# Statistic rows of stage 3: one split operand and one product of 64 rows for each spread, in place of a product of 5 fp32 rows

## The reference, cut to what matters

```python
o = _rmsnorm(o, gla_norm_g) * silu(r)          # each of 4 heads of 128 channels by itself
u = silu(_layernorm(conv(u), conv_ln_g, conv_ln_b))   # 512 channels
x = x + gt1 * concat([o, u]) @ w_out
h = _rmsnorm(x, norm_ffn_g) * (1 + sc2) + sh2   # then router logits, then the experts
```

## Time and profile before

| | us |
|---|---|
| median of 3 runs | 2720.18 |
| the three runs | 2714.88, 2720.18, 2720.66 |
| the profiled execution, its own time | 2712.45 |
| span of its instructions | 2709.8 |
| stage 3, from about 848 to 1322 in the span | 474 |

### The profile page before, as it was taken

How to read it: one execution, slowest core, us unless ns; L and a number is a source line. 1 busy time by engine, 2 the same in 40 slices (tenths; PEclk the granted TensorE clock), 3 DMA queues, 4 the chain that set the end, 5 groups by cost and what they waited for, 6 DMA issues and landing times.

```text
span 2709.8 us, 41042 instructions
## 1 busy us (share of the span) xinstructions
PE 2461.4 (91%) x15405; PEld 2166.3 (80%) x15405; DVE 1624.5 (60%) x2729; ACT 1208.0 (45%) x1946; POOL 782.2 (29%) x686
## 2 busy tenths in 40 slices
PE   5679989999997889999649999999999999999994
PEld 1667868688785566777418999999999999999994
DVE  0575949679496453342464666665566666665575
ACT  3555355464423233323115555555544555555553
POOL 1020010101000031101012554445555544445451
PEclk9879989999997879889658999999999999999997
DMA  5884565665545446432444766667777666666875
GB/s 194 304 289 159 172 214 190 232 199 183 198 164 204 132 140 163 121 113 84 128 87 141 207 194 191 192 184 205 198 199 206 194 195 195 183 196 198 285 230 202
DMA packets 287074, 505.61 MB, mean 187 GB/s; under 512 B 31614, under 2 KB 230107, under 8 KB 271098
## 3 DMA queue, kind: packets, MB, share of 16 engines
q1 hardware_dynamic: 247562, 377.84, 42.4%
q0 software_dynamic: 39408, 126.38, 17.8%
HBM read 405.63 MB, written 98.53 MB: 186 GB/s over the span
## 4 chain that ended last, share of the span: by engine, by line
PE 77%; DVE 6%; ACT 4%; DMA 3%; issue 2%; POOL 2%; SPq 0%; DVEq 0%; ACTq 0%; POOLq 0%
PE bank L1423 22%; PE bank L1425 22%; PE bank L1424 22%; PE bank L1606 2%; PE bank L1544 1%; DVE work_out L2079 1%; PE bank L1672 1%; PE bank L1637 1%; PE bank L1583 1%; PE bank L1571 1%; DVE work_exp L2272 1%; ACT work_proj L747 1%; PE bank L1663 1%; DMA out_dram<-work_exp 1%; PE bank L1484 1%
## 5 line engine op out<-in xcount | busy, mean ns | idle before, releaser
L1423 PE MATMUL bank<-act_hl_exp,hl_exp 128*128 128x288 f32 x3072 | 913.0, 297 | 38.3 <-POOL act_hl_exp L1341 25.3
L1424 PE MATMUL bank<-act_hl_exp,hl_exp 128*128 128x288 f32 x3072 | 909.2, 296 | 0.0
L1425 PE MATMUL bank<-act_hl_exp,hl_exp 128*128 128x288 f32 x3072 | 907.5, 295 | 0.0
L1423 PEld LDWEIGHTS bank<-act_hl_exp,hl_exp 128*128 128x128 f32 x3072 | 579.0, 188 | 42.0 <-issue 30.3
L1425 PEld LDWEIGHTS bank<-act_hl_exp,hl_exp 128*128 128x128 f32 x3072 | 581.3, 189 | 0.0
L1424 PEld LDWEIGHTS bank<-act_hl_exp,hl_exp 128*128 128x128 f32 x3072 | 580.2, 189 | 0.0
L2390 DVE TENSOR_TENSOR hl_exp<-work_exp,hl_exp 128x1024 fp32r<-128x1024 f32 x192 | 231.7, 1227 | 226.4 <-ACT hl_exp L1030 226.4
L2390 DVE TENSOR_TENSOR hl_exp<-raw_exp,hl_exp 128x1024 fp32r<-128x1024 f32 x192 | 232.3, 1225 | 201.9 <-ACT hl_exp L1030 201.9
L2032 DVE SCALAR_TENSOR_TENSOR work_proj<-work_proj,wcv 128x392 f32<-128x392 f32 (+11 forms) x600 | 343.2, 644 | 0.0
L1030 ACT ACTIVATE hl_exp<-work_exp 128x1024 fp32r<-128x1024 f32 x192 | 199.5, 1055 | 217.8 <-PE bank L1425 212.6
L1030 ACT ACTIVATE hl_exp<-raw_exp 128x1024 fp32r<-128x1024 f32 x192 | 198.6, 1052 | 166.4 <-PE bank L1425 166.4
(11 more groups left out here) (320 smaller groups left out, 3642.8 us busy)
## 6 DMA issues: line engine op xcount, KB each, us to landing
hl_proj<-park_w POOLq DMA_DIRECT2D x80, 1024.0 KB, 5.5
raw_exp<-in_w_e_gate_dram SPq DMA_DIRECT2D x32, 1024.0 KB, 5.7
raw_exp<-in_w_e_up_dram SPq DMA_DIRECT2D x32, 1024.0 KB, 5.7
work_exp<-in_w_e_gate_dram SPq DMA_DIRECT2D x32, 1024.0 KB, 6.2
work_exp<-in_w_e_up_dram SPq DMA_DIRECT2D x32, 1024.0 KB, 5.8
raw_exp<-in_w_e_down_dram SPq DMA_DIRECT2D x32, 1024.0 KB, 5.6
work_exp<-in_w_e_down_dram SPq DMA_DIRECT2D x32, 1024.0 KB, 5.7
park_w<-hl_proj SPq DMA_DIRECT2D x10, 2048.0 KB, 12.5
```

The costliest lines, as they stand in the source:

```text
L1423: pe.matmul(out, lh, rh, start=first, stop=False)
L1424: pe.matmul(out, lh, rl, start=False, stop=False)
L1425: return pe.matmul(out, ll, rh, start=False, stop=last_)
```

## The change

ACT copies the five reciprocals as fp32r (high part) to rows 0 to 4 of a 64-row tile, and DVE writes what the copy left out (low part) to rows 32 to 36. The other rows are zero. The stationary operand of product h has ones in rows h and 32 + h (`spread_sel`), so that one fp32r product adds both parts; before it was a product of two fp32 operands of 5 rows. The tile lies in `reset`, which POOL clears for it at the start of stage 3. `spread` waits for the low part instead of the reciprocals. The rest of the diff moves counts of the semaphore `r_sel`.

```diff
+        spread_rs = reset.bitcast(f32r)[0:64, 0:BT]
+        spread_sel = reset.bitcast(f32r)[0:64, BT:BT + 5]
...
+        r_sh, r_sl = s_zt.again(0), s_z.again(0)
...
+            def stat_hi(m):
+                act.wait_ge(r_rc, m + 1)
+                wait_pos(act, r_bc, 5 * m)
+                if m == 0:
+                    act.wait_ge(r_sel, 7)
+                act.activation(spread_rs[0:5, 0:T3[m]], W3["rs"][0:5, 0:T3[m]], ACT.Copy).then_inc(r_sh.sem, 1)
...
                 if prep:
                     stat_roots(prep)
+                    stat_hi(prep)
                 if NT3[m] == 4:
                     evict(g0 + 1)
...
+            pool.memset(reset[0:64, 0:2 * BT], 0.0).then_inc(r_sel, 1)
             pool.memset(W3["selc"], 0.0).then_inc(r_sel, 1)
-            pool.wait_ge(r_sel, 1)
+            pool.wait_ge(r_sel, 2)
...
             def spread(m):
-                pe.wait_ge(r_rc, m + 1)
+                upto(pe, r_sl, m + 1)
...
-                    pe.matmul(psum[6 + h % 2][:, 0:T3[m]], ident[0:5, h:h + 1].broadcast_to([5, 128]), W3["rs"][0:5, 0:T3[m]], start=True,
-                              stop=True).then_inc(r_bc, 1)
+                    pe.matmul(psum[6 + h % 2][:, 0:T3[m]], spread_sel[:, h:h + 1].broadcast_to([64, 128]),
+                              spread_rs[:, 0:T3[m]], start=True, stop=True).then_inc(r_bc, 1)
...
-                pe.wait_ge(r_sel, 6)
+                pe.wait_ge(r_sel, 7)
...
                 dve.reciprocal(rs, rs).then_inc(r_rc, 1)
+                upto(dve, r_sh, m + 1)
+                dve.tensor_tensor(spread_rs[32:37, 0:T3[m]], rs, spread_rs[0:5, 0:T3[m]].bitcast(f32), ALU.subtract)\
+                   .then_inc(r_sl.sem, 1)
...
             def prologue():
+                dve.tensor_tensor(spread_sel, ident[0:64, 0:5], ident[0:64, 32:37], ALU.add)
```

More of the change, by code:

```diff
@@ L372, in hybrid_layer @@
         e_dn, e_yt, e_yev, e_sc = sem("e_dn"), sem("e_yt"), sem("e_yev"), sem("e_sc")
-        e_mod, e_row = Sig(r_sel, 0, 0, 6), Sig(r_nst, 0, 0, 16)
+        e_mod, e_row = Sig(r_sel, 0, 0, 7), Sig(r_nst, 0, 0, 16)
         e_u = sem("e_u")
@@ L383, in hybrid_layer @@
         f_s3 = Sig(k_m, 0, 0, 33)
-        f_q, f_g = Sig(k_cnt, 0, 0, CNT_IL + 3), Sig(r_sel, 0, 0, 6 + 96)
+        f_q, f_g = Sig(k_cnt, 0, 0, CNT_IL + 3), Sig(r_sel, 0, 0, 7 + 96)
         f_gl = sem("f_gl")
@@ L972, in prologue @@
                 stat_roots(0)
+                stat_hi(0)
                 cat_his(0)
```

## The result

The changed kernel takes 2697.02 us (median of 8 runs, 2689.96 to 2705.06), the kernel before 2716.47 us in 8 runs beside it. The ratio is 0.9934, 95% interval 0.9917 to 0.9951: about 18 us faster, where 10.6 us (0.9961) had been forecast and 2701 was the low end of the range. The first three runs of the kernel before, on whose median of 2720.18 the forecast was built, were 3.7 us slower than the median of all eight.

The account below looks back on a forecast made before the run. PE bounds the kernel, its chain covering 77% of the span. Blocks 2 to 4 gain 8.2 us with three falls, block 1 1.6; three falls 9.8, two 11.4, middle 10.6: 2720.18 - 10.6 = 2709.6 us, range 2701 to 2718.

Parts of the forecast that it names:

- the old stretch: Blocks 2 to 4, from the spread's first product to the router behind it: 12.13, 13.55 and 13.58 us before.
- I expect one fall behind it in two or three of the three blocks: Blocks 2 to 4: clock drops to 1.2 GHz behind the new 3.2 us spread; total gain 9.8 to 11.4 us, chance 0.60.
- first rival: Blocks 2 to 4: the clock stays up; gain 14.5 us, giving 2705.7 us; chance 0.15.
- the middle of the forecast: Whole kernel: 10.6 us gain, between 9.8 with three falls of the clock and 11.4 with two.
- Block 1: Split uncovered: first product 1.4 us later, last scaling 1.5 earlier, parked states cap the gain at 1.7; 1.6 us taken.
- That a product of 64 rows takes what one of 128 does: Each new fp32r spread product takes 0.23 us, the figure for 128 rows; bounds 0.23 and 0.43.
- The split is covered: Blocks 2 to 4: copy and subtraction, 1.4 us, finish 1.0 us before PE asks for the low part.
- Block 0: Split adds about 0.8 us, products give about as much back, ahead of a 10.55 us wait for parked states: zero.
- Clearing the tile: POOL at the start of stage 3: 0.9 us, upper bound 1.8, ahead of a wait for a DMA: zero.
- ACT's chain: Behind the spread: silus, copies and `token` run 10.7 us until PE's `row_T`; the gain is handed on.
- The clock by rule: Skill's rule that long idle gaps drop the clock: new spread's gaps, under 0.7 us, would keep it; the old trace disagrees.

Follow-up runs that it names:

- the split alone: Kernel before plus the split, made and waited for but unused; each spread still a product of 5 fp32 rows from the reciprocals: ratio 1.0008.
- The padded kernel: Kernel before with its five fp32 rows written into a cleared tile of 64 rows, without the split: ratio 0.9972.
- the woven run: Changed kernel with the five spread products laid between the 24 products of the projection behind, blocks 2 to 4: 2698.79 us, ratio 0.9943.
- the tucked run: Changed kernel with 128 rows, products 0 and 1 ahead of the transposes, 2 to 4 each behind three projection products: 2707.90 us, ratio 0.9918.

## Why the prediction was wrong, point by point

**Where the gain lies.** All in stage 3. Three profiles of each kernel:

| | stage 3, us | its start, us | stretches of blocks 2, 3, 4, us |
|---|---|---|---|
| before | 473.9, 484.2, 479.6 | 848.5, 844.5, 842.1 | 12.13, 13.55, 13.58; 12.14, 15.21, 15.21; 13.57, 13.55, 13.56 |
| after | 459.5, 457.0, 466.0 | 839.8, 845.9, 840.4 | 8.70, 8.67, 10.25; 8.67, 8.67, 10.26; 8.70, 8.68, 8.67 |

The means are 479.3 and 460.8: 18.5 us, which is the whole measured difference; outside stage 3 the three spans of each kernel differ by 2 us in the mean (2243.7 and 2241.6). The start scatters in both, and in the eight profiles of the other kernels, with the same code ahead of it (841.7 to 848.1).

**The step that failed: sizing the old stretch from one execution.** The 12.13 us of block 2 and the 13.55 and 13.58 of blocks 3 and 4 were right for that execution and mild for the kernel. Over nine stretches the mean is 13.6, with two of 15.2. The prediction had seen that a fall of the clock costs 1.5 us or 3, and did not ask how often the costly case comes; it had one execution, but three of three stretches with a fall should have opened the range on the side of a larger gain.

**The step beside it: "I expect one fall behind it in two or three of the three blocks", because PE is idle for two thirds.** There was one in two of nine (10.25 and 10.26). Idle time alone was the wrong thing to look at. The count of rows of the products counts too, as the kernels side by side show:

| product | rows | stretches with a fall in the spread or right behind it |
|---|---|---|
| two fp32 instructions | 5 | 12 of 12 (three profiles of before, one of the split alone) |
| two fp32 instructions | 64 | 0 of 6 |
| one fp32r | 5 | 2 of 3 |
| one fp32r | 64 | 2 of 9 |
| one fp32r | 128 | 0 of 6 |

The three stretches of a profile are not independent draws. For fp32 the times confirm the table: both kernels with 64 rows are faster than the kernel before beyond their intervals. For fp32r the counts are too small to tell 5 rows from 64 or 64 from 128. So the forecast's first rival, the clock staying up, was nearly what happened, at 2 of 9. Its words "products of 64 rows in place of 5" named the cause without giving it the weight.

**What each step is worth.** Blocks 2 to 4 gave 14.9 us (mean time from the start of the spread of block 2 to the end of stage 3: 294.4 before, 279.5 after), where the middle of the forecast had 9.0 (8.2 with a fall in each, 12.9 with none). The stretches hold 3 x (13.61 - 9.03) = 13.7 of it. Of these 4.7 above the forecast, 1.6 are the old stretches (40.8 us for three, not 39.3) and 2.9 the falls that did not come (0.7 in an execution, not 2.5, at 1.6 each); the remainder is rounding (the forecast's three gains with a fall add up to 8.4 before they are rounded) and a stretch of 8.7 in place of 8.8. The other 1.2 us lie in where later falls land. All this holds for means of three: the 294.4 stands for 291.4, 299.0 and 292.9, the 279.5 for 278.2, 278.2 and 282.3. The forecast in microseconds also set out from 2720.18; the kernel before has 2716.47 over eight runs, and 2716.47 - 10.6 = 2705.9 leaves 8.9 us to the measured 2697.02.

**Block 1.** Step by step it came as written, against the first profile: from the start of the reciprocals the first product is 4.78 us away against 3.39, 1.4 later; the last scaling ends 8.65 us away against 10.17, 1.5 earlier; L2073 (now L2086) starts 14.38 away against 16.10, 1.7 earlier, held by the DMA. But that too was sized against one execution, with the clock still up at the start of the old spread. In the other two profiles of before the last scaling ended 11.37 us away, so that the change gains 2.7 there. The mean time from the start of stage 3 to the spread of block 2 fell by 3.6 us (184.8 to 181.3), not 1.6; single profiles of one kernel scatter by 4 to 5 us in it, so that of this only the direction is shown.

**Right only roughly.** That a product of 64 rows takes what one of 128 does: the first two are 0.34 us apart where 0.23 had been written, the projection starts 0.42 us behind product 4 (0.34 with 128 rows), and the stretch is 8.67 us (8.45 with 128 rows). It cost the forecast little, since VectorE paces the spread.

**Right as written.** The spread 3.10 us (3.2), the stretch 8.7 with the clock up (8.8) and 10.25 with one fall (10.3). The split is covered by 1.02 us (1.0) and costs nothing measurable. Block 0: the spread began 39.4 us after the start of stage 3, against 38.9 (means of three). Clearing the tile took 0.94 us (0.9), the selection 0.16. ACT's chain handed the gain on: the transposes came 3.4 us earlier behind the spread of block 2 (1040.69 - 1021.08 = 19.6 against 23.04).

**The clock by rule.** The Trainium skill (TensorE: Matmul & The Clock Gate, section "Why this matters for your kernels") warns of long idle gaps. The padded kernel and the kernel before have the same instructions at the same pace and the same gaps, and differ in the clock, so the rule in that form doesn't explain what these runs show.

**What stays open.** Why the later fall, some 12 or 20 us behind the spread, lands where it does in an execution. It moves stage 3 by several us (457.0 to 466.0 in three profiles of one kernel), and it was not tried. Open too is whether the number of rows counts by itself at the fp32r rate, and how many rows are enough at the fp32 rate: only 5 and 64 were run. And no run shows why rows of zeros keep the clock up.

## What to carry to other kernels

A thin product can cost time behind itself: 5 fp32 rows against 64 cost this kernel 7 us through the clock of the spread's end and of the dense products that follow, and padding with zeros gets them back. Where a trace shows the clock falling in or behind a stretch, treat the length of that stretch as one draw of several, and put the dearer cases into the range. To weave small products into dense ones, place them so that their consumer gets each at the time it did before; in the woven run, where it got them later, the work behind the consumer took the gain back.

## What the runs showed of the hardware that was not expected

- The granted clock fell in or right behind a spread of fp32 products of 5 rows in 12 of 12 stretches, and in none of 6 with the same instructions over 64 rows; in three of these six, 59 of the rows were zeros.
- A product of 64 rows between products of 128 costs more than its 0.23 us. In the woven run such a product started 0.32 us after the product ahead and the next 0.42 us after it (timeline of block 2):

```profile
1030.66 0.39 PE L1438 MATMUL bank<-wo_hl,cat_hl 128*128 128x512 f32 x1
...
1030.98 0.50 PE L1650 MATMUL bank<-reset 64*128 64x512 f32 x1
...
1031.40 0.50 PE L1436 MATMUL bank<-wo_hl,cat_hl 128*128 128x512 f32 x1
```

  With 128 rows in the tucked run the two steps are 0.24 and 0.24:

```profile
1208.04 0.40 PE L1438 MATMUL bank<-wo_hl,cat_hl 128*128 128x512 f32 x1
...
1208.28 0.40 PE L1650 MATMUL bank<-reset 128*128 128x512 f32 x1
...
1208.52 0.39 PE L1436 MATMUL bank<-wo_hl,cat_hl 128*128 128x512 f32 x1
```
